# A planned kernel with other planning numbers and deadlines, and a rewritten last output projection

## What is computed

```python
x = layer_norm(x, ln0_g, ln0_b)
q, k, v, z_a, bg, cg, h, z_c = jnp.split(jnp.einsum('bsd,de->bse', x, w_in), 8, axis=-1)
y_att = chunk_attention(heads(q), heads(k), heads(v), rel_bias) * silu(z_a)
y_conv = bg * conv3(cg * h) * silu(z_c)
y = concatenate([y_att, y_conv], -1)
x = layer_norm(ALPHA * x + einsum('bse,ed->bsd', y, w_out), ln_g, ln_b)
```

## Time and profile before

| | us |
|---|---|
| median of the runs | 1320.6 |
| lowest run | 1318.0 |
| the profiled execution, its own time | 1315.5 |
| span of the slowest core (core 2) in it | 1313.9 |
| span of core 0 in it | 1313.1 |
| TensorE busy, core 0 | 1276.7 |
| DVE, ScalarE, POOL busy, core 0 | 941.8, 730.6, 534.0 |

### The profile page before, as it was taken

How to read it: one execution, slowest core, us unless ns; L and a number is a source line. 1 busy time by engine, 2 the same in 40 slices (tenths; PEclk the granted TensorE clock), 3 DMA queues, 4 the chain that set the end, 5 groups by cost and what they waited for, 6 DMA issues and landing times.

```text
span 1313.9 us, 27380 instructions; the slowest of 8 cores (1311.1 to 1313.9 us)
## 1 busy us (share of the span) xinstructions
PE 1264.3 (96%) x8146; PEld 594.9 (45%) x8308; DVE 943.1 (72%) x1671; ACT 731.4 (56%) x1082; POOL 529.5 (40%) x880
## 2 busy tenths in 40 slices
PE   5989999999999999999999999999999999999996
PEld 3434444444444444444444444444444444444443
DVE  2488987858678685876858688585885868676377
ACT  4665555555545565654654556465564565555563
POOL 4555533424343342433524334243443334334244
PEclk9999999999999999999999999999999999999998
DMA  9993313323222331222312323131222313221012
GB/s 290 322 254 113 88 55 93 89 49 89 58 77 79 87 89 25 88 83 73 89 41 73 89 74 96 59 87 41 83 87 73 89 43 89 69 76 49 13 70 73
DMA packets 126001, 117.16 MB, mean 89 GB/s; under 512 B 103200, under 2 KB 103200, under 8 KB 125728
## 3 DMA queue, kind: packets, MB, share of 16 engines
q1 hardware_dynamic: 125856, 115.40, 30.8%
HBM read 57.69 MB, written 33.55 MB: 69 GB/s over the span
## 4 chain that ended last, share of the span: by engine, by line
PE 89%; issue 3%; DMA 3%; DVE 2%; POOL 2%; ACT 1%; SPq 1%; POOLq 0%; DVEq 0%; ACTq 0%
PE mm L646 45%; PE mm L657 17%; PE mm L760 15%; PE pv L967 6%; PE sc L911 5%; DMA cst_sb<-cst 1%; DMA out<-xs 1%; DMA xs<-x 1%; DMA xnT<-xhb 0%; PE mm L833 0%; POOL pvs L985 0%; DVE stats L528 0%; DVE PT L951 0%; ACT xhb L855 0%; POOL rstd L538 0%
## 5 line engine op out<-in xcount | busy, mean ns | idle before, releaser
L646 PE MATMUL mm<-xnT,w_in_sb 128*128 128x512 bf16 x2970 | 709.3, 379 | 9.2 <-DVE tz L710 3.7
L646 PEld LDWEIGHTS mm<-xnT,w_in_sb 128*128 128x128 bf16 x3072 | 285.5, 98 | 300.6 <-issue 29.5
L924 ACT ACTIVATE PT<-sc 128x1024 bf16<-128x1024 f32 (+1 forms) x288 | 275.9, 999 | 115.6 <-PE sc L911 110.9
L657 PE MATMUL mm<-w_in_sb,xnT 128*128 128x512 bf16 x996 | 237.9, 379 | 1.9 <-issue 1.1
L760 PE MATMUL mm<-w_out_sb,yT 128*128 128x512 bf16 x929 | 221.5, 379 | 1.9 <-issue 1.3
L967 PE MATMUL pv<-vA,PT 128*128 128x65 bf16 x2240 | 203.3, 193 | 10.8 <-POOL PT L936 3.8
L967 PEld LDWEIGHTS pv<-vA,PT 128*128 128x128 bf16 x2240 | 150.2, 97 | 126.2 <-issue 18.6
L951 DVE TENSOR_TENSOR PT<-PT,etab 128x512 bf16<-128x512 bf16 (+1 forms) x304 | 123.6, 429 | 95.2 <-POOL PT L936 51.9
L985 POOL TENSOR_TENSOR pvs<-pvs,rden 128x256 f32<-128x256 f32 x128 | 100.7, 786 | 193.3 <-DVE rden L984 152.4
L657 PEld LDWEIGHTS mm<-w_in_sb,xnT 128*128 128x128 bf16 x1024 | 95.4, 98 | 105.7 <-issue 9.5
L766 DVE SCALAR_TENSOR_TENSOR xs<-xs,mm 128x512 f32<-128x512 f32 x120 | 82.2, 685 | 70.1 <-PE mm L760 59.1
(11 more groups left out here) (88 smaller groups left out, 1147.1 us busy)
## 6 DMA issues: line engine op xcount, KB each, us to landing
xs<-x SPq DMA_DIRECT2D x64, 512.0 KB, 3.6
out<-xs SPq DMA_DIRECT2D x60, 512.0 KB, 2.8
xs<-w_in SPq DMA_DIRECT2D x20, 512.0 KB, 12.8
g1bc_sb<-w_in SPq DMA_DIRECT2D x4, 512.0 KB, 12.7
b1bc_sb<-w_in SPq DMA_DIRECT2D x4, 512.0 KB, 12.8
vA<-w_in SPq DMA_DIRECT2D x4, 512.0 KB, 13.1
yT<-ytok SPq DMA_TRANSPOSE x128, 2.3
out<-xs SPq DMA_DIRECT2D x8, 256.0 KB, 2.0
```

Of the source, the lines that this page charges most:

```text
L646: P.op("pe", lambda e, i=i, kc=kc: e.matmul(mm[i][:, :], lhsT=w_in_sb[:, kc, c0:c0 + 128], rhs=xnT[:, sl, kc, :], start=(kc == 0), stop=(k ...
L657: P.op("pe", lambda e, i=i, kc=kc, t=t, c0=c0: e.matmul(mm[i][:, :], lhsT=xnT[:, sl, kc, t * 128:(t + 1) * 128], rhs=w_in_sb[:, kc, c0:c0 ...
L924: P.op("act", lambda e, x=x, sp=sp, w=w: e.activation(out=PT[:, sp, :, 0:w], in_=sc[x][:, :, 0:w], func=AF.Exp, scale=0.125), reads=["sc%d ...
```

## The change

Planning numbers: an operation now holds its engine for its duration plus an offset by engine (HOLD: ScalarE -0.09, DVE -0.08, POOL +0.17 us); the latency from one engine to the next is 0.145 us to TensorE, 0.16 where POOL takes part, else 0.1; DMA moves 0.31 MB per us, 0.235 at the start; all engines are free from 1.0 us on. The planned durations of the small POOL steps and of the bias product grow. An operation that nothing needs is due 8 us behind TensorE's end at the latest.

One choice: the memset of PT may run on POOL or on DVE. In the plan that results, 107 stand on POOL and 85 on DVE; of the 40 weight casts ScalarE has 19 where it had 7.

Last block: the projection is written tile by tile (o_last). Tile 0 runs seven matmuls for each of its halves and then the eighth of both. Tiles 1 and 2 are as before. The last tile is done in pieces of 512, 256 and 256 columns, each with a DVE add and bn_stats; bn_aggr then gives mean and variance, DVE centres, POOL makes rstd, and DVE closes both halves, each with its store. ScalarE takes no part in the last tile.

```diff
-LAT = 0.1
-DMA_MB = 0.3
+HOLD = {"pe": 0.0, "act": -0.09, "dve": -0.08, "pool": 0.17, "sp": 0.0}
+
+
+def lat(a, b):
+    if b == "pe":
+        return 0.145
+    return 0.16 if "pool" in (a, b) else 0.1
+
+
+DMA_MB = 0.31
 PASSES = 3
...
     def op(self, eng, fn, reads=(), writes=(), us=0.2, fill=False):
-        self._add(eng, fn, reads, writes, us, us + (0.17 if eng == "pe" else 0.0))
+        self._add(eng, fn, reads, writes, us + HOLD[eng], us + (0.17 if eng == "pe" else 0.0))
...
-                n["alap"] = min(n["alap"], n["at"] + 60.0)
+                n["alap"] = min(n["alap"], n["at"] + 60.0, t + 8.0)
...
-                gap = 0.0 if n["eng"] == "pe" and nd["eng"] == "pe" else nd["lat"] + LAT + (SLACK if n["eng"] == "pe" else 0.0)
+                gap = 0.0 if n["eng"] == "pe" and nd["eng"] == "pe" else (
+                    nd["lat"] + lat(nd["eng"], n["eng"]) + (SLACK if n["eng"] == "pe" else 0.0))
...
-        free = {e: 0.0 for e in ENGS}
+        free = {e: 1.0 for e in ENGS}
...
-            return n["choices"][e][1] if n["eng"] is None else n["us"]
+            return n["choices"][e][1] + HOLD[e] if n["eng"] is None else n["us"]
...
-                dmaq = max(dmaq, s + 0.9) + n["mb"] / DMA_MB
+                dmaq = max(dmaq, s + 0.9)
+                dmaq += n["mb"] / (DMA_MB if dmaq > 9.5 else 0.235)
...
-                    ready[m] = max(ready[m], end + LAT)
-                    solid[m] = max(solid[m], end + LAT)
+                    r = end + lat(e, nodes[m]["eng"])
+                    ready[m] = max(ready[m], r)
+                    solid[m] = max(solid[m], r)
...
-             reads=["mv0_%d" % u], writes=["rstd0_%d" % u])
+             reads=["mv0_%d" % u], writes=["rstd0_%d" % u], us=0.35)
...
-             reads=["rstd0_%d" % u, "nhalf"], writes=["rstd0_%d" % u], us=0.57)
+             reads=["rstd0_%d" % u, "nhalf"], writes=["rstd0_%d" % u], us=0.65)
...
-                 reads=["halo%d" % cc], writes=["uh%d" % (cc % 2)], us=0.3)
+                 reads=["halo%d" % cc], writes=["uh%d" % (cc % 2)], us=0.4)
...
-    def unit_O_last(b, t, hf):
+    def o_mm(b, t, i, c0, w, chunks, first, last):
+        for n, c in enumerate(chunks):
+            assert (yc_of[c - 4] if c >= 4 else yt_of[c // 2, t]) == b
+            P.op("pe", lambda e, c=c, n=n: e.matmul(
+                mm[i][:, 0:w], lhsT=yT[:, c, t * 128:(t + 1) * 128], rhs=w_out_sb[:, c, c0:c0 + w],
+                start=(first and n == 0), stop=(last and n == len(chunks) - 1)),
+                reads=["w_out%d" % c, ("yT%d_%d" % (c // 2, t)) if c < 4 else "yT%d" % c],
+                writes=["mm%d" % i], us=w / 2400.0 + 0.0024)
+            pos_now[0] += 1
+            pump_pv(3)
+
+    def o_last(b):
+        order = (4, 5, 6, 0, 1, 2, 3, 7)
+        pair = [next_mm(), next_mm()]
+        for hf in range(2):
+            o_mm(b, 0, pair[hf], hf * 512, 512, order[:7], True, False)
+        for hf in range(2):
+            o_mm(b, 0, pair[hf], hf * 512, 512, order[7:], False, True)
+            o_sum(b, 0, hf, pair[hf])
+        ln1_last(b, 0)
+        for t in (1, 2):
+            for hf in range(2):
+                i = next_mm()
+                o_mm(b, t, i, hf * 512, 512, order, True, True)
+                o_sum(b, t, hf, i)
+            ln1_last(b, t)
+        t = TPB - 1
+        s = slot_of(b, t)
+        for k, (c0, w) in enumerate(((0, 512), (512, 256), (768, 256))):
+            i = next_mm()
+            o_mm(b, t, i, c0, w, order, True, True)
+            P.op("dve", lambda e, i=i, c0=c0, w=w: e.tensor_tensor(
+                out=xs[:, s, c0:c0 + w], in0=xs[:, s, c0:c0 + w], in1=mm[i][:, 0:w], op=ALU.add),
+                reads=["mm%d" % i, "xs%d" % s], writes=["xs%d" % s], us=t_dve(w))
+            P.op("dve", lambda e, k=k, c0=c0, w=w: e.bn_stats(
+                out=stats0[:, k // 2, k % 2, :], in_=xs[:, s, c0:c0 + w]),
+                reads=["xs%d" % s], writes=["stats0_%d" % (k // 2)], us=t_dve(w))
+        ln1_end(b, t, s)
+
+    def ln1_end(b, t, s):
+        n = b * TPB + t
+        P.op("dve", lambda e: e.bn_aggr(out=mv0[:, 0, :], in_=stats0[:, 0:2, :, :].rearrange(
+            "p u a b -> p (u a b)")[:, 0:18]),
+            reads=["stats0_0", "stats0_1"], writes=["mv0_0"], us=0.22)
+        P.op("pool", lambda e: e.tensor_scalar(out=rstd0[:, 0:1], in0=mv0[:, 0, 1:2], scalar1=LN_EPS,
+                                               scalar2=None, op0=ALU.add),
+             reads=["mv0_0"], writes=["rstd0_0"])
+        P.op("pool", lambda e: e.tensor_tensor(out=rstd0[:, 0:1], in0=rstd0[:, 0:1], in1=nhalf[:, 0:1], op=ALU.pow),
+             reads=["rstd0_0", "nhalf"], writes=["rstd0_0"], us=0.57)
+        P.op("dve", lambda e: e.scalar_tensor_tensor(
+            out=ybuf[:, t, :], in0=xs[:, s, :], scalar=mv0[:, 0, 0:1], in1=g1bc[:],
+            op0=ALU.subtract, op1=ALU.mult),
+            reads=["xs%d" % s, "mv0_0", "g1bc"], writes=["y%d" % t], us=1.28)
+        for h, nm in ((0, "xa"), (1, "xb")):
+            c = slice(512 * h, 512 * h + 512)
+            P.op("dve", lambda e, c=c: e.scalar_tensor_tensor(
+                out=xs[:, s, c], in0=ybuf[:, t, c], scalar=rstd0[:, 0:1], in1=b1bc[:, c],
+                op0=ALU.mult, op1=ALU.add),
+                reads=["y%d" % t, "rstd0_0", "b1bc", "xs%d" % s], writes=["%s%d" % (nm, s)], us=0.75)
+            P.dma("sp", lambda e, c=c: e.dma_start(out=out_d[n][:, c], in_=xs[:, s, c]), "st%s%d" % (nm[1], t),
+                  reads=["%s%d" % (nm, s)], mb=0.25)
+
+    def o_sum(b, t, hf, i):
         s = slot_of(b, t)
         xr_ = ["xs%d" % s]
-        i = next_mm()
-        order = (4, 5, 6, 0, 1, 2, 3, 7)
-        for n, c in enumerate(order):
-            assert (yc_of[c - 4] if c >= 4 else yt_of[c // 2, t]) == b
-            P.op("pe", lambda e, i=i, c=c, n=n: e.matmul(
-                mm[i][:, :], lhsT=yT[:, c, t * 128:(t + 1) * 128],
-                rhs=w_out_sb[:, c, hf * 512:(hf + 1) * 512], start=(n == 0), stop=(n == 7)),
-                reads=["w_out%d" % c, ("yT%d_%d" % (c // 2, t)) if c < 4 else "yT%d" % c],
-                writes=["mm%d" % i], us=0.2157)
-            yield
-        P.op("dve", lambda e, i=i: e.scalar_tensor_tensor(
+        P.op("dve", lambda e: e.scalar_tensor_tensor(
             out=xs[:, s, hf * 512:(hf + 1) * 512], in0=xs[:, s, hf * 512:(hf + 1) * 512], scalar=1.0,
             in1=mm[i][:, :], op0=ALU.mult, op1=ALU.add, accum_out=sums[:, t, hf:hf + 1]),
             reads=xr_ + ["mm%d" % i], writes=xr_ + ["sum%d_%d" % (t, hf)], us=0.8)
-        if hf == 1:
-            ln1_last(b, t)
 
     def ln1_last(b, t):
...
-                    P.op("pool", lambda e, sp=sp, c0=c0: e.memset(PT[0:64, sp, :, c0:c0 + 64], 0.0),
-                         writes=rs, us=0.2)
+                    fn = lambda e, sp=sp, c0=c0: e.memset(PT[0:64, sp, :, c0:c0 + 64], 0.0)
+                    P.any_op({"pool": (fn, 0.2), "dve": (fn, 0.2)}, writes=rs)
...
-            reads=rs + ["etab"], writes=rs, us=t_dve(2 * n, 2.0))
+            reads=rs + ["etab"], writes=rs, us=t_dve(2 * n, 2.0) + 0.06)
...
-    run_units([unit_O_last(nblk - 1, t, hf) for t in range(TPB) for hf in range(2)])
+    run_events(pos_now[0] + 1)
+    o_last(nblk - 1)
```

12 lines of the change are left out of this document (6 added, 6 removed).

## The result

The changed kernel is slower: 1366.5 us against 1319.3 us in the median, a ratio of 1.037 (95%: 1.036 to 1.039), where I had forecast 1312.0 us. Each of the two medians is over four executions, one of them in a slower state of the chip (1542.8 and 1518.7 us), and the ratio leaves those two out. The profiled execution took 1365.8 us. Its page is of core 7, the slowest, whose trace holds all 8316 matmuls. Core 7 spans 1364.1 us at a mean granted clock of 0.986; in the kernel before it spanned 1312.1 us at 0.998.

What follows compares the result with a forecast made beforehand. TensorE, busy 97% of the span with full steady blocks, was taken as the bound; 2.0 (head and first waits) + 1.3 + 1.3 + 2.2 + 0.1 = 6.9 us gave 1312 us, range 1304 to 1321.

Steps and rivals of the forecast that it cites:

- Head (a): Start of the kernel: rstd pairs ahead of weight casts bring the last transposes 2.0 us earlier, at most 2.0 gained.
- Waits to 120 us (a, b): Head and TensorE waits from 66 to 120 us: 2.0 kept of 4.8, plus 1.3 at an evacuation, 1.3 at memsets.
- The tz waits: Near 73 and 82 us, TensorE waiting for DVE's tz step: 2.8 us expected to go, partly taken back later.
- The second block's first projection: Behind the tz waits: a short wait expected, taking back part of the up to 4.8 us freed before it.
- the two waits that were to be under 1 us: At 97.91 (evacuation, 2.27 us) and 114.14 (memsets, 1.68 us): each under 1 us, 1.3 gained at each.
- Later waits (c): TensorE's waits on PT tiles after 120 us: 2.2 of 3.7 us gained, under 2 us left in sum.
- the steady blocks are full: From 640 to 1240 us TensorE is busy for all 600 us, so no order of other engines shortens them.
- Memsets: 85 PT memsets moved to DVE: 0.2 us each, 17 us over the span, no cost where DVE is idle.
- The slower rival: Memset or bias product on DVE behind a 1.28 to 2.21 us step: about 1.3 us per uncovered place; chance 0.1.
- Last block: Last projection to the end: yT wait of 0.5 us goes, end 25.5 us in, 0.1 us gained for both edits.

Runs made afterwards that it cites:

- e13: Changed kernel with ScalarE's list altered in the head alone: three evacuations of the first block's transposes ahead of a weight cast; 1363.0 us.
- e6: Changed kernel with SyncE's queue altered alone: each x load ahead of the yT transposes right in front of it; 1337.8 us.
- e3: Changed kernel with every planner number set back to the kernel before; memset choice and new last block stay; 1341.7 us.
- e7: e3 with GpSimd's list altered alone: a memset right behind a tile's first rstd step now stands ahead of it; 1323.0 us.
- e4: Kernel before with the new last block alone, all planner numbers old and memsets on GpSimd; 1317.0 us.
- e9: Changed kernel with HOLD at zero and the planned margin ahead of a probability product at 1.5 us for 0.6; 1327.6 us.
- e5: Changed kernel with VectorE's list altered at nine places: bias products ahead of residual affine b; 1358.7 us.
- e12: Changed kernel with one planner number changed: a transposing DMA booked on SyncE for 1.7 us (1.15 before); 1328.4 us.

## Why the prediction was wrong

- **Head (a).** The events came where I put them: last transposes 16.72 us (16.7 forecast), first projection 17.85 (18). The 2.0 us were not kept on this core: z_a starts at 34.96 as before. I looked for what could be late next among the weights and left out ScalarE's list, where a weight cast now stands ahead of the evacuations (e13). Across the cores z_a starts between 32.5 and 35.0 us: later than 33.8 on the five where the wait for the evacuation was followed by 0.50 of the clock, before 32.9 on the other three.
- **Waits to 120 us (a, b).** The tz waits went, as forecast. The second block's first projection waits 3.34 us, not "short", and the two waits that were to be under 1 us are 1.90 (evacuation) and 2.62 (memset), with a new one of 1.63 on a bias product. Of the 4.6 us that I booked up to there (2.0, 1.3, 1.3) nothing came, and 6.0 us were lost by the 385th matmul.
- **Later waits (c).** "Under 2 us in sum" is 27 us. The step that failed is "the steady blocks are full, and no order of the other engines can make them shorter". No kernel here shortened them, but I took the fullness of the old order for a property of any order, and put a loss there at nothing. The steady blocks lost 46.3 us, at nine waits of 2.2 to 3.2 us and the lower clock behind five of them; with the x load alone put on time, 28.7 us come back (e6). The planner leaves some 0.6 us between a tile and its product, and steps come up to 3 us late; the lists of before have few places where the two meet.
- **Memsets.** On VectorE a memset takes 165 ns in the mean, less than the 0.2 us I put down, and 14 us over the span that VectorE had to spare. The cost is in what it did to the order: 24.7 us (e3), of which 18.7 come back when memset and rstd step change places again (e7). I had the rule that speaks for it: the Trainium skill, SBUF — State Buffer, "Who interferes with whom", says that a GpSimd step that reads SBUF and a VectorE step with two SBUF inputs exclude each other while a pure write is not touched. The rows of e3 and e4 agree (rstd step 1.05 and 0.73 us beside the affine, memset 0.20), and I let the 2.2 us of (c) stand against it.
- **The slower rival** named the mechanism, a bias product or memset behind a step of 1.28 us in front of a product, and then sized it wrongly: 1.3 us a place where the trace shows 2.2 to 3.2 and, at five of the nine, some 3 to 6 us at half the clock behind it. Its chance of 0.1 rested on the old lists waiting nowhere, which says nothing of new ones.
- **Last block.** Right. The wait on yT is gone, the matmuls take 14.0 us, the aggregate ends at 1358.04, 19.1 us in (19.0 forecast), the first rstd step of the last tile runs ahead of the centring step and the second beside it, to 0.4 us past its end (I had put both behind it), and the end comes 25.2 us in (25.5 forecast, 25.6 before):

```profile
1338.92 14.00 PE L840 MATMUL mm<-w_out_sb,yT 128*128 128x512 bf16 x72
...
1357.81 0.23 DVE L878 BATCH_NORM_AGGREGATE mv<-stats 128x2 f32<-128x18 f32 x1
...
1358.58 1.64 POOL L884 TENSOR_TENSOR rstd<-rstd,nhalf 128x1 f32<-128x1 f32 x1
```

What stays open: why the ten orders planned here with another number or choice, that of the change among them, are all 10 us or more slower than that of before was not settled; nor was what holds the 21 us by which e6 is still above e4; and the price of broken score runs in e9 was read, not isolated.

## What to carry to other kernels

Where a planner sets in-order lists, a new table of numbers is a new program: price it not by the waits that are left in the old order but by how late the steps can be (here loads by 3 us, GpSimd steps by 1) against the margin that the plan leaves in front of the bounding engine (0.6 us). Look for the work with slack that waits for a late transfer at the head of an in-order list, and mend the lateness (e6: 29 us), not the one step that is seen to wait (e5: 8 us). A number that makes a better plan is not shown to be the right number (e12: 38 us by booking more than the step takes); alter one list and leave the others to learn what an order costs. And TensorE busy without a break is no proof of the same pace: count its instructions in the window too.

## What the runs showed of the hardware

On core 7 of the changed kernel a single idle stretch of 2.2 to 3.2 us in an otherwise full TensorE was followed, at five of nine places, by some 3 to 6 us at the granted clock of 0.50, with the engine busy nearly all that time (843.2 to 849 us); at the other four it stayed at 1.00. Over all eight cores it fell behind 51 of the 72 waits at these places, and their length does not tell which: behind a wait of 1.97 us it fell, behind one of 3.02 it did not. A transposing DMA of yT holds SyncE's queue for 1.16 us in the median, two in a row mostly for some 2.46 us and now and then for 3.2 to 3.6, so a load behind them leaves that much later. Beside a VectorE affine of 1.28 us a 128x1 step of GpSimd that takes 0.2 us at the least took up to 1.31 us, and a memset 0.20 as ever.
